# Gate and up products by seven block products in place of eight, from the seventh tile on, in a two-layer hybrid trunk

## What is computed

```python
def swiglu(x, w_gu, w_down):
    gate, up = jnp.split(x @ w_gu, 2, axis=-1)
    return (jax.nn.silu(gate) * up) @ w_down

for l in range(DEPTH):                       # DEPTH = 2
    x = x + 0.5 * rmsnorm(swiglu(rmsnorm(x, n[0]), w1_gu[l], w1_down[l]), n[1])
    m, S_a, S_r = mixer(rmsnorm(x, n[2]), ...)   # gated linear attention and retention heads
    x = x + rmsnorm(m, n[3])
    x = x + 0.5 * rmsnorm(swiglu(rmsnorm(x, n[4]), w2_gu[l], w2_down[l]), n[5])
```

## Time and profile before

| | us |
|---|---|
| median of 3 runs (2232.84 to 2233.83) | 2233.33 |
| span of the profiled execution | 2232.8 |
| PE busy | 2201.3 (99% of the span) |
| POOL busy | 941.5 (42%) |
| ACT busy | 820.4 (37%) |
| DVE busy | 811.5 (36%) |

### The profile page before, as it was taken

One profiled execution on the slowest core, in us unless ns is written; L12 is line 12 of the kernel. 1 busy time (PEld: TensorE's weight loads), 2 busy tenths in 40 slices (PEclk: granted clock), 3 DMA queues, 4 the chain that ended last, 5 costly groups with the idle time before them and its releaser, 6 DMA issues.

```text
span 2232.8 us, 43710 instructions
## 1 busy us (share of the span) xinstructions
PE 2201.3 (99%) x17863; PEld 2176.0 (97%) x17863; DVE 811.5 (36%) x1146; ACT 820.4 (37%) x1443; POOL 941.5 (42%) x776
## 2 busy tenths in 40 slices
PE   8999999999999999999999999999999899999998
PEld 8999999999989999999999999999999899999998
DVE  4222200577367422220162222006863873222102
ACT  4333333442344433332353333335424453333323
POOL 3444444443315444444444444444532344444442
PEclk9999999999999999999999999999999999999999
DMA  6223222322234223223323222233322443222232
GB/s 177 87 85 91 76 84 87 89 78 79 70 86 142 76 85 92 86 68 91 115 68 91 87 85 74 84 92 82 86 67 57 118 117 94 85 85 86 75 91 72
DMA packets 381054, 197.60 MB, mean 89 GB/s; under 512 B 8868, under 2 KB 379352, under 8 KB 380824
## 3 DMA queue, kind: packets, MB, share of 16 engines
q1 hardware_dynamic: 363856, 185.89, 28.9%
q10 hardware_dynamic: 17096, 10.24, 1.6%
HBM read 186.80 MB, written 9.31 MB: 88 GB/s over the span
## 4 chain that ended last, share of the span: by engine, by line
PE 94%; DVE 4%; ACT 1%; issue 1%; DMA 0%; SPq 0%; ACTq 0%; DVEq 0%
PE ps L542 88%; PE ps L740 1%; DVE x L1520 1%; DVE y L1514 1%; DVE xs_lo L1457 0%; PE ps L902 0%; PE ps L919 0%; PE ps L814 0%; ACT o_hi L1336 0%; DMA x_tok<-in_x_prompt_dram 0%; PE ps L569 0%; ACT xs_hi L1081 0%; PE ps L841 0%; PE ps L781 0%; PE ps L582 0%
## 5 line engine op out<-in xcount | busy, mean ns | idle before, releaser
L477 POOL TENSOR_TENSOR w_lo<-raw,w_hi 128x512 fp32r<-128x512 f32 (+1 forms) x708 | 878.9, 1246 | 1139.8 <-ACT w_hi L1108 1139.8
L542 PE MATMUL ps<-xs_hi,w_hi 128*128 128x288 f32 (+1 forms) x3616 | 767.2, 289 | 4.4 <-DVE xs_lo L1457 4.2
L542 PE MATMUL ps<-xs_hi,w_lo 128*128 128x288 f32 (+1 forms) x3616 | 765.6, 288 | 0.0
L542 PE MATMUL ps<-xs_lo,w_hi 128*128 128x288 f32 (+1 forms) x3616 | 762.9, 288 | 0.0
L1108 ACT ACTIVATE w_hi<-raw 128x512 fp32r<-128x512 f32 (+1 forms) x708 | 410.2, 585 | 956.5 <-PE ps L542 955.7
L542 PEld LDWEIGHTS ps<-xs_hi,w_hi 128*128 128x128 f32 x3616 | 588.4, 189 | 11.1 <-DVE xs_lo L1457 6.2
L542 PEld LDWEIGHTS ps<-xs_lo,w_hi 128*128 128x128 f32 x3616 | 588.0, 189 | 0.2
L542 PEld LDWEIGHTS ps<-xs_hi,w_lo 128*128 128x128 f32 x3616 | 584.6, 188 | 0.0
L1478 DVE TENSOR_TENSOR tmp<-ps,rstd_pre 128x544 f32<-128x544 f32 x88 | 63.8, 725 | 633.2 <-PE ps L542 613.8
L542 PE MATMUL ps<-h_hi,w_lo 128*128 128x256 f32 x1272 | 267.2, 289 | 0.0
L542 PE MATMUL ps<-h_lo,w_hi 128*128 128x256 f32 x1272 | 266.1, 288 | 0.0
(11 more groups left out here) (220 smaller groups left out, 1836.2 us busy)
## 6 DMA issues: line engine op xcount, KB each, us to landing
raw<-in_w_gu_dram SPq DMA_DIRECT2D x176, 512.0 KB, 3.8
raw<-in_w_in_dram SPq DMA_DIRECT2D x56, 512.0 KB, 3.8
raw<-in_w_down_dram SPq DMA_DIRECT2D x64, 384.0 KB, 3.4
raw<-in_w_down_dram SPq DMA_DIRECT2D x64, 320.0 KB, 3.1
raw<-in_w_out_dram SPq DMA_DIRECT2D x16, 512.0 KB, 3.9
ret_state<-in_state_ret_dram SPq DMA_DIRECT2D x8, 512.0 KB, 6.0
out_dram<-ret_state ACTq DMA_DIRECT2D x8, 512.0 KB, 5.2
gla_state<-in_state_gla_dram SPq DMA_DIRECT2D x4, 512.0 KB, 7.4
```

The source lines that it names most:

```text
L477: pool.tensor_tensor(lo, raw[:, u, k0:k0 + n, :], hi.bitcast(F32), ALU.subtract)\
L542: mm = pe.matmul(bank_part(bank, a), w, v[:, kx, TOK[a]], start=(start and n == 0), stop=(stop and n == 2))
```

## The change

In each feed-forward block the first 6 gate and up tiles stay as they are (`PLAIN_GROUPS = 3`, `TILE0 = 6`). The other 16 (`NPAIR`) are computed by Winograd's form of Strassen's product. The weight of one pair is cut into four blocks, input rows in halves of 4 tiles and columns into gate and up; the tokens are cut into halves of 272. In place of eight block products there are seven terms, each over 4 tiles with three matmuls: 84 matmuls of 272 columns for a pair, in seven PSUM banks, one for each term.

- **Inputs.** Terms need sums of inputs, so the inputs are normed first: `norm_inputs` writes x * gain * rstd_pre into `xn` (8 instructions on DVE behind tile 1), `input_sum` makes four sums of 4 x 272 columns, and `xb_split` (ACT) and `xb_low` (DVE) split the seven inputs into `xb`, behind tiles 2 and 3 and in the first window.
- **Weights.** For each pair DVE makes four sums of weight blocks (`term_sum`, 128x512 each). ACT rounds the seven terms (`term_split`), POOL makes the low parts of terms 0 and 1, and DVE those of terms 2 to 6 (`term_low`).
- **Results.** ACT copies term 0 out of PSUM (`keep`), and DVE takes six steps (`take_c`), five of 272 columns and one of 544, to get gate and up; silu, product, `h_hi` and `h_lo` follow as before, without the scaling by `rstd_pre`.
- **Space.** `xb` reaches over the places of h's low parts for hidden tiles 10 to 20. Their low parts go to DRAM (`send_away`, 272 KB each, SP's queue) and come back in three DMAs (`fetch`) once terms 0, 1 and 2 of the last window are done; the low parts lie turned by 12 places (`turn=LATE`). Tables (cos, sin, masks) share space with the late sums and are loaded again in the middle of each first down stage. A memset of `s_gla` moves from the start of the kernel into the mixer.
- **Loops.** The windows are written out, no longer hardware loops.

```diff
+            def pair_terms(l, f, n):                       # PE
+                i = f * NPAIR + n
+                for j, c_ in enumerate(TERM_INPUTS):
+                    wait_term(pe, l, f, n, j)
...
+                    elif j == 0:
+                        wait(pe, kept_ready, l, i - 1)
+                    else:
+                        wait_c(pe, l, f, n - 1, ("c11", "u2", "u4_c22", "u3", "c12", "c21")[j - 1])
+                    for k in range(KH):
+                        for m, (w, part) in enumerate(((term_hi, 0), (term_hi, 1), (term_lo, 0))):
+                            mm = pe.matmul(ps[:, j, 0:TH], w[j][:, k, :], xb[:, c_, part, k, :],
+                                           start=(k == 0 and m == 0), stop=(k == KH - 1 and m == 2))
+                    mm.then_inc(term_done.sem, 1)
...
+            def pair_window(l, f, n):                      # ACT
...
+                    term_split(l, f, n, 6)
+                    pair_high(l, f, n - 1)
+                    keep(l, f, n)
...
+                    for j in range(5):
+                        term_split(l, f, n + 1, j)
...
+                silu_pair(l, f, n)
+                if more:
+                    term_split(l, f, n + 1, 5)
...
+            def pair_window(l, f, n):                      # DVE
+                more = n + 1 < NPAIR
+                if n:
+                    take_c(l, f, n - 1, "c21")
+                    term_low(l, f, n, 6)
+                    pair_product(l, f, n - 1)
+                    if more:
+                        term_sum(l, f, n + 1, 1)
+                    pair_low(l, f, n - 1)
+                    take_c(l, f, n, "c11")
+                    take_c(l, f, n, "u2")
...
+                if more:
+                    term_sum(l, f, n + 1, 2)
+                    term_sum(l, f, n + 1, 4)
+                    term_low(l, f, n + 1, 2)
+                take_c(l, f, n, "u3")
+                take_c(l, f, n, "u4_c22")
+                if more:
+                    term_sum(l, f, n + 1, 3)
+                    term_low(l, f, n + 1, 3)
+                take_c(l, f, n, "c12")
+                if more:
+                    term_low(l, f, n + 1, 4)
+                    term_low(l, f, n + 1, 5)
```

More of the change, by code:

```diff
@@ L37 @@
 LEVELS = (64, 32, 16, 8, 4, 2, 1)
+PLAIN_GROUPS = 3
+TERM_INPUTS = (4, 5, 6, 0, 1, 2, 3)
+C_ORDER = ("c11", "u2", "u3", "u4_c22", "c12", "c21")
 class Signal:
@@ L261, in c @@
             a, b = cc[name]
-            return cst[0:parts, a:b]
+            return tab[0:parts, a - TAB0:b - TAB0] if a >= TAB0 else cst[0:parts, a:b]
+        term_hi = [w_hi[:, j] for j in range(SPLIT_SLOTS)] + [late_hi[:, 0], late_hi[:, 1], last_hi[:, :, :]]
+        term_lo = [w_lo[:, j] for j in range(SPLIT_SLOTS)] + [late_lo[:, j] for j in range(NTERM - SPLIT_SLOTS)]
+        kept, u_2, u_3 = rstd_pre[:, 0:TH], acc[:, 0:TH], acc[:, TH:T]
+        h_away = nc.dram_tensor("h_away", [2 * DEPTH, P, NAWAY, T], F32).ap()
         ident, ones, eps = c("ident"), c("ones"), c("eps")
@@ new lines, in ffn @@
+                load_next(l, f, 2, 0, w_gu, w_down)
+                for n in range(NPAIR):
+                    load_next(l, f, n + 2, 1, w_gu, w_down)
+                    if AWAY0 <= TILE0 + n - 1 < AWAY1:
+                        send_away(l, f, TILE0 + n - 1)
+                    if n + 3 < NPAIR + 2:
+                        load_next(l, f, n + 3, 0, w_gu, w_down)
+                for part in range(3):
+                    fetch(l, f, part)
+                with sp.Fori(1, DOWN_GROUPS // 2) as m:
+                    k_parts(l * GROUPS + DOWN[f] + m, w_down, l, bass.ds(m * P, P), DOWN_KT)
@@ L1155, in pre_norm, with plain_tile @@
                 act.activation(rstd_pre[:, :], rstd_pre[:, :], ACT.Exp, scale=-0.5).then_inc(pre_ready.sem, 1)
[L1157 to L1165, removed]
+            def plain_tile(l, f, t):
+                wait(act, gate_scaled, l, f * TILE0 + t)
+                act.activation(tmp[:, 0, :], tmp[:, 0, :], ACT.Silu).then_inc(gate_silu.sem, 1)
@@ L1470, in add_x_squares @@
                        .then_inc(xsq_step.sem, 1)
-            def up(l, f):
[L1473 to L1489, removed]
@@ new lines, in plain_low, with norm_inputs @@
+            def plain_low(l, f, t):
+                wait(dve, hh_ready, l, f * KF + t)
+                dve.tensor_tensor(low_place(t), tmp[:, 0, :], h_hi[:, t, :].bitcast(F32), ALU.subtract)\
+                   .then_inc(h_ready.sem, 1)
+                wait(dve, h_ready, l, f * KF + t)
+            def norm_inputs(l, f):
+                for k in range(KD):
+                    half = slice(2 * (k // KH), 2 * (k // KH) + 2)
+                    dve.scalar_tensor_tensor(out=xn[:, half, k % KH, :], in0=x[:, k, :].rearrange("p (h t) -> p h t", h=2),
+                                             scalar=gain(l, 4 * f, k),
+                                             in1=rstd_pre[:, :].rearrange("p (h t) -> p h t", h=2),
+                                             op0=ALU.mult, op1=ALU.mult).then_inc(xn_ready.sem, 1)
```

378 lines of the change are left out of this document (342 added, 36 removed).

## The result

| | before | after |
|---|---|---|
| median of 20 runs, us (lowest to highest) | 2233.58 (2232.22 to 2234.76) | 2237.0 (2236.19 to 2237.64) |
| span of the profiled execution, us | 2232.8 | 2234.9 |

The ratio is 1.0016, with a 95% interval of 1.0009 to 1.0023: 3.4 us slower where 9.6 us faster were forecast. The time lies inside the predicted range and inside rival A's own (2210 to 2238). The step is small, but it is clear of noise, since the interval leaves out 1, and it goes the other way than was forecast.

The account below looks back on a forecast made before the run. The kernel before was taken as bound by PE's matmul count, with DVE becoming the bound: 9.21 + 0.69 + 1.03 + 0.21 + 0.74 = 11.88 us a window, 9.6 us gained, median 2223.7 us, range 2187 to 2256.

Parts of the forecast that it names:

- rival A: Feed-forward windows bound by DVE just under the old period: 11.88 us against 12.06, 2210 to 2238 us; chance 0.57.
- POOL's hold: Two POOL low parts block DVE instructions with two SBUF inputs, delaying sums 2 and 4: +0.69 and +1.03 us a window.
- the wait for term 5: In each window DVE idles before term 5's low part, since ACT has silu ahead of its split: +0.74 us.
- the wait for h_hi: In each window DVE idles before h's low part until ACT's copy into h_hi is done: 0.21 us.
- The signs named in the prediction: 768 fewer matmuls, DVE near 11 of 11.9 us busy, PE waits on w_lo and late_lo, sums 2 and 4 long.
- the price of an instruction that needs the result of the one before: In DVE's window a dependent instruction starts 0.03 us after its predecessor's end, adding 0.115 us at u3 and u4.
- the way by DRAM: Low parts fetched back for the first down tile land at 10, 13 and 16 us, before PE's need: zero cost.
- B: PE stays the bound in the windows, POOL's hold and both waits being covered: window 10.54 us, 2147 us; chance 0.08.
- C: POOL's first instruction in a window falls wholly under PSUM reads, saving 0.69 us: period 11.19, 2185 us; chance 0.11.
- D: POOL's first starts 0.5 us later, sum 4 and low part 2 take full holds: period 12.45, 2255 us; chance 0.23.
- E: PE's idle gaps in the windows throttle its clock to 1.2 GHz: window near 20 us, 500 us slower; chance 0.01.

Follow-up runs that it names:

- e4: The change without the product of low weight and high input in all seven terms (56 matmuls a window in place of 84): 2237.5 us.
- e1: The change with the low parts of terms 0 and 1 moved from POOL to DVE from the third pair on: 2205.2 us.
- e3: The change with the low parts of terms 0 and 1 left out, POOL only signalling (result not valid): 2145.6 us.
- e2: The change with ACT splitting term 5 ahead of silu: 2192.0 us.
- e9: The change with e1's and e2's edits, dependent pairs separated, pair 1's low parts on DVE, c11 ahead of h's low part, keep ahead of h_hi: 2147.9 us.
- e8: The change with only sum 3 moved between u3 and u4_c22: 2223.7 us.

## Why the prediction was right and wrong

**Right: DVE becomes the bound.** 9.21 us of instructions plus POOL's hold plus two waits for ACT. e4 shows that PE doesn't set the time, e1 and e3 the hold, e2 the wait for term 5, e9 the wait for h_hi. The signs named in the prediction are all there, but for one: in the windows behind the first PE waits for `w_lo` alone, of POOL at term 0 and of DVE at term 3, and never for `late_lo`.

**Right: the layout of the window.** Counted from the start of c21, forecast against trace: h's low part 2.41, 2.40 (126.89 - 124.49); sum 2 ends 5.07, 5.08; low part 2 can start at about 6.7, 6.70; low part 5 starts 11.28, 11.36. The wait for h_hi shows as 0.81 between sum 1 and h's low part (126.08, 126.89), 0.21 over 0.60; the wait for term 5 as 1.33 between the starts of low parts 4 and 5 (134.52, 135.85), 0.73 over 0.60, where 0.74 was written.

**Wrong: the size, since all three terms of the sum were too short.** The step that failed is the price of an instruction that needs the result of the one before, taken as 0.03 us behind its end and measured as 0.11 to 0.20, and with it the start of the first window, where DVE comes late out of a hold by POOL. Three things are added up for a block; measured in the first one:

| term | forecast | trace |
|---|---|---|
| PE's start of window 0 (92.20) to c21 (112.50) | 19.15 | 20.30 |
| 14 periods | 166.3 (11.88) | 167.6 (11.97) |
| last c21 (280.13) to PE's down stage (285.38) | 4.96 | 5.25 |
| sum | 190.5 | 193.2 |

Before it was 192.9; the other three blocks take 193.2, 193.1 and 193.5. The terms are short by 6%, 0.8% and 6%, or 4.6, 5.2 and 1.2 us over four blocks. DVE's timeline at both ends of the block:

```profile
91.63 1.57 DVE L1817 TENSOR_TENSOR sum<-raw,sums_early 128x512 f32<-128x512 f32 x1
93.12 0.71 DVE L1751 TENSOR_TENSOR tmp<-ps,rstd_pre 128x544 f32<-128x544 f32 x1
...
104.91 0.68 DVE L1807 TENSOR_TENSOR sum<-raw 128x512 f32<-128x512 f32 x1
105.79 0.69 DVE L1811 TENSOR_TENSOR sums_early<-sum,raw 128x512 f32<-128x512 f32 x1 [0.20 <-DVE sum L1807]
106.62 0.69 DVE L1817 TENSOR_TENSOR sum<-raw,sums_early 128x512 f32<-128x512 f32 x1
...
283.51 0.43 DVE L1833 TENSOR_TENSOR acc<-ps,rstd_pre 128x272 f32<-128x272 f32 x1
284.05 0.44 DVE L1836 TENSOR_TENSOR acc<-ps,acc 128x272 f32<-128x272 f32 x1
284.60 0.72 DVE L1839 TENSOR_TENSOR tmp<-ps,acc 128x544 f32<-128x544 f32 x1
```

The first term fell short by 1.15. DVE's last plain scale (L1751) should have started some 0.2 behind PE's end of the tile at 92.20; sum 4, another one that POOL held, was still on DVE, and it started at 93.12, 0.92 behind. In e3, where POOL holds nothing, it starts 0.27 behind. Later sums 1, 2 and 4 follow each other, each in need of the one before, at 0.88 and 0.83 in place of 0.60.

The second term is the price of a dependent neighbour, which was taken as 0.03 behind the end of the one before, from the earlier trace rows. Here it is 132.33 - (131.79 + 0.43) = 0.11 at u4_c22, which makes 0.07 of the 0.09 that a period is longer. At sum 4 it is 129.70 - (128.23 + 1.34) = 0.13, but that costs the steady window nothing, since sum 4 ends behind POOL in any case.

The pair in the earlier trace rows was read rightly: in `rotate` the second instruction adds to what the first one wrote, and all 16 such pairs start 0.03 behind, in the kernel after too. It was the wrong pair to go by. One difference stands in the code: `rotate` has one wait between the two, for the first one's own semaphore, u3 and u4_c22 have two (PE's term and the step before), sum 4 three and sum 2 four, and the distances are 0.03, 0.11, 0.13 and 0.20. That the waits make the difference is argued and not shown; no run takes one away. e8 shows the price itself.

The third term is the same restart, at u3 and at u4_c22 (0.54 and 0.55 between the starts).

The forecast span was 2223.2, the measured one is 2234.9: 11.7 apart, of which these 2.7 us a block make 10.8. (By the table's rows the forecast is 190.4; the prediction rounded up.) One small piece of the rest: the first block's plain tiles end 0.4 later than before, 0.2 of it a wait of PE for POOL's low part, since xb's long instructions on DVE hold POOL there (four of POOL's take 8.00 us in place of 5.1), which was written off as hidden. The other 1.6 us between forecast and median are the distance of a median from the span of one execution, taken as 0.5 and here 2.1. The 0.5 was misread: it laid a median of three beside the span of another execution. Where both are on record for one execution, the launch is 1.8 us above the span, in every run (here 2236.72 and 2234.9). Against before, the delay can be followed through the kernel at ACT's eviction of the first down tile (L1206 before, L1480 after): 301.44 and 302.25 in the first block, 1402.53 and 1403.94 in the third, 2101.76 and 2103.93 in the fourth.

**Right: no price for the way by DRAM, as far as the trace goes.** The fetches are issued from 283.71 on, and the median of those of 1088 KB lands after 6.7 us, of the last ones, 816 KB, after 9.7; PE's wait list has none on `h_lo` in the first down tile, and its tiles follow each other at the old pitch of 16.57 us. A run with that way lengthened or removed was not made.

**The rivals.** B (2147) didn't occur, but is the time that e9 reaches (2147.9) once the hold and the waits are gone and PE is the bound. C (2185) fell with sum 2's 1.34 us in each window. D didn't occur either: the period stopped at 11.97, short of its 12.05, and the kernel is slower even so. The 12.05 was worked out with the forecast edges; with the measured ones the two kernels are level at (192.9 - 20.30 - 5.25) / 14 = 11.95. D's own sum doesn't come out as written either: 2 x 1.15 + 2 x 0.14 in place of 1.72 gives 12.74 and not 12.45. E's clock stayed at 1.00. In all, the forecast gain was 2.4 us a block, the small difference of two sums near 190. Its sign was not to be had from terms that were good to 0.1 us each; the range said so, the forecast value didn't. That 2237.0 still fell inside A's own range, by 1 us, is luck in part: 17 errors of 0.03 make 0.12 a window if they fall at random and 0.51 if all go one way, and the 0.25 that gives the range was a choice between the two.

## What to carry to other kernels

When a change takes work from one engine and gives it to another, write out the receiving engine's window instruction by instruction, with dependent neighbours, port holds and the other engines' order in it: here that gave the window within 1% of its length. If the sum comes out near the old time, the gain is in where and in what order the instructions run: the same work, in another order and with POOL's low parts on DVE, took 89 us off. Keep instructions that need the result of the one before apart, keep GpSimd off SBUF while VectorE is full, and after each move ask whose input just got later.

## What the runs showed of the hardware

- A VectorE instruction that reads the result of its predecessor starts 0.03 us after that one's end in the mixer's pairs and 0.11 to 0.20 us after it in the windows; independent ones start 0.08 before it. At 0.11 that is 0.19 us more than the 0.35 that a 272-column instruction costs.
- VectorE and GpSimd take turns when a VectorE instruction with two SBUF inputs and one of GpSimd are both waiting: the GpSimd pair is stretched from 2.56 to 2.98 us, the VectorE pair from 1.20 to 2.96, of which 0.21 is a restart that GpSimd has no part in. VectorE instructions that read PSUM and one SBUF operand kept their 0.35 beside it.
- TensorE's granted clock was 0.85 of full on average in a stretch of e4 in which it was busy for 79% of the time and idle for 2.1 us once a window, and the kernel's time didn't change; at 94% busy, with gaps of up to 0.5 us in each window, it stayed at 1.00.
